# Expert layer: choice of the first two tiles stretched by 1.3 and moved apart, gate products later, row products on a straighter curve

## What is computed

```python
qh = (x2 @ w_q).reshape(t, 8, 2, 128)
scores = einsum('thcd,hckd->thck', qh, sub_keys)          # 8 heads x 2 halves x 128 keys
sv, si = top_k(scores, 16)
cand = sv[..., 0, :, None] + sv[..., 1, None, :]          # 16 x 16 sums for each head
cv, ci = top_k(cand, 16)                                  # 16 experts for each head
experts = i1 * 128 + i2                                   # of 16384
gates = softmax(cv)
act = gelu(einsum('tkd,td->tk', expert_u[experts], x))
out = einsum('tk,tkd->td', act * gates, expert_v[experts])
```

## Time and profile before

| | |
|---|---|
| Median of 3 runs | 3953.37 us (3952.84 to 3953.43) |
| Profiled execution, its own time | 3957.06 us |
| Its span, first to last instruction | 3955.3 us |
| Mean granted TensorE clock | 0.990 |
| TensorE matmuls | busy 3844.4 us, 97% |
| TensorE weight loads | 85% |
| VectorE | busy 2453.7 us, 62% |
| ScalarE | 39% |
| GpSimd | 14% |
| Up-projection stage | about 740 to 1500 us of the span |

### The profile page before, as it was taken

One profiled execution on the slowest core, in us unless ns is written; L12 is line 12 of the kernel. 1 busy time (PEld: TensorE's weight loads), 2 busy tenths in 40 slices (PEclk: granted clock), 3 DMA queues, 4 the chain that ended last, 5 costly groups with the idle time before them and its releaser, 6 DMA issues. The chain is left out here.

```text
span 3955.3 us, 53100 instructions
## 1 busy us (share of the span) xinstructions
PE 3844.4 (97%) x21989; PEld 3357.1 (85%) x21989; DVE 2453.7 (62%) x3730; ACT 1531.9 (39%) x2178; POOL 550.4 (14%) x405
## 2 busy tenths in 40 slices
PE   8999998998999999999999999999999999999998
PEld 7778887788999999999988887788888887688887
DVE  6433478699889767778775525765444542685443
ACT  3211345324766753333342226543222233644222
POOL 1000101101233333343311100110001010001000
PEclk9999999999999999999999999999999999999999
DMA  3344135335898999999944443332223434143332
GB/s 128 110 129 159 47 106 182 112 112 189 275 319 295 350 347 350 354 358 358 354 178 151 133 138 110 113 111 96 96 96 107 141 130 146 67 143 101 97 99 81
DMA packets 294188, 689.52 MB, mean 174 GB/s; under 512 B 19731, under 2 KB 77459, under 8 KB 277052
## 3 DMA queue, kind: packets, MB, share of 16 engines
q1 hardware_dynamic: 247868, 526.72, 39.4%
q0 software_dynamic: 36864, 134.23, 9.7%
q10 hardware_dynamic: 9216, 25.17, 1.6%
HBM read 585.11 MB, written 100.96 MB: 173 GB/s over the span
## 5 line engine op out<-in xcount | busy, mean ns | idle before, releaser
L1328 ACT CAST pe_w_high<-pe_w_raw 128x2048 fp32r<-128x2048 f32 (+1 forms) x168 | 316.4, 1883 | 601.7 <-DMA pe_w_raw<-in_peer_v_units 347.8
L1420 DVE TENSOR_TENSOR pe_w_low<-pe_w_raw,pe_w_high 128x2048 fp32r<-128x2048 f32 (+1 forms) x168 | 382.2, 2275 | 269.2 <-ACT pe_w_high L1328 269.0
L1215 PE MATMUL ps<-xn_p_high,pe_w_high 128*128 128x384 f32 (+1 forms) x1088 | 379.9, 349 | 17.7 <-DVE pe_w_low L1420 16.5
L2335 ACT CAST tail_w_high<-tail_w_raw 128x2048 fp32r<-128x2048 f32 (+3 forms) x124 | 221.4, 1790 | 442.0 <-DMA tail_w_raw<-in_w_in 144.5
L2344 DVE TENSOR_TENSOR tail_w_low<-tail_w_raw,tail_w_high 128x2048 fp32r<-128x2048 f32 (+3 forms) x124 | 266.7, 2155 | 184.5 <-ACT tail_w_high L2335 184.2
L1215 PE MATMUL ps<-xn_p_low,pe_w_high 128*128 128x384 f32 (+1 forms) x1088 | 371.1, 341 | 0.0
L1215 PE MATMUL ps<-xn_p_high,pe_w_low 128*128 128x384 f32 (+1 forms) x1088 | 371.0, 341 | 0.0
L1245 PE MATMUL ps<-pe_far_hidden_high,pe_w_high 128*128 128x384 f32 x1024 | 342.7, 335 | 0.0
L1245 PE MATMUL ps<-pe_near_hl,pe_w_high 128*128 128x384 f32 x1024 | 342.1, 334 | 0.0
L1245 PE MATMUL ps<-pe_far_hidden_high,pe_w_low 128*128 128x384 f32 x1024 | 342.1, 334 | 0.0
L1633 POOL DMA_INDIRECT home_pe_row<-in_peer_u,pe_expert x128 | 174.6, 1364 | 558.7 <-DVE pe_act L1606 361.6
(11 more groups left out here) (649 smaller groups left out, 9069.3 us busy)
## 6 DMA issues: line engine op xcount, KB each, us to landing
pe_w_raw<-in_peer_u_units SPq DMA_DIRECT2D x64, 1024.0 KB, 7.3
pe_w_raw<-in_peer_v_units SPq DMA_DIRECT2D x64, 1024.0 KB, 7.9
in_w_raw<-in_w_in SPq DMA_DIRECT2D x34, 1024.0 KB, 5.7
tail_w_raw<-in_w_up SPq DMA_DIRECT2D x32, 1024.0 KB, 5.5
tail_w_raw<-in_w_down SPq DMA_DIRECT2D x32, 1024.0 KB, 5.0
pe_w_raw<-in_w_in SPq DMA_DIRECT2D x28, 1024.0 KB, 5.0
tail_w_raw<-in_w_in SPq DMA_DIRECT2D x28, 1024.0 KB, 4.9
dram_peer_hidden<-pe_rings_r ACTq DMA_DIRECT2D x64, 384.0 KB, 5.8
```

The source lines that it names most:

```text
L1215: last = pe.matmul(ps[:, q, 0:n], w[:, s, at], xp[:, 4 * i + c, 0:n], start=(i == 0 and c == 0 and p == 0), stop=(i == 1 and c == 3 and p ...
L1328: act.copy(ring.flat(hi, u), ring.flat(raw, u)).then_inc(w_hi, 1)
L1420: dve.tensor_tensor(ring.flat(lo, u), ring.flat(raw, u), ring.flat(hi, u).bitcast(F32), ALU.subtract).then_inc(w_lo, 1)
L2335: act.copy(hi, raw).then_inc(self.w_hi, 1)
```

## The change

It changes seven planned numbers, or forms of them, and splits one semaphore.

- The choice of tile 0 begins at start(8) + 82 instead of + 70 (180.0 instead of 168.0 planned). Tile 3 stays at 128.0.
- Tiles 3 and 0 get the pace 1.3 instead of 1.0, and the exponentials follow the pace: 28.4 behind the start of the choice instead of 22 for tiles 3 and 0, 46.4 instead of 50 for tiles 1 and 2.
- The gate iterations run from 231.0 to 670.4 planned, 9.35 apart, instead of from 206.0 to 666.0, 9.79 apart. Through them tile 1's choice moves from 262.6 to 280.6 and tile 2's from 419.2 to 430.2, and the stores of the table move along.
- The exponent in `DOT` is 0.9 instead of 0.8: of the 128 row products, more come early and fewer late.
- `gate_stored` becomes two semaphores, one for each output buffer, with the waits on it rewritten.

`turns` is not among the changed lines. The due times of the units, of the loads, of the low halves and of the sums of rows stay. The whole diff:

```diff
--- before.py
+++ after.py
@@ -1030,13 +1030,14 @@
     ORDER = (3, 0, 1, 2)
     TURNED = [m for m in ORDER if m * P < N_DENSE]
     N_TURNS = len(TURNED)
-    PICK = {3: start(8) + 30.0, 0: start(8) + 70.0}
-    GATE = lambda it: PICK[0] + 38.0 + (start(D0) - 46.0 - PICK[0] - 38.0) / n_gates * it
+    PICK = {3: start(8) + 30.0, 0: start(8) + 82.0}
+    GATE = lambda it: PICK[0] + 51.0 + (start(D0) - 42.0 - PICK[0] - 51.0) / n_gates * it
     PER_BURST, N_BURSTS = BURST // UNIT, N_DENSE // BURST
     for m in (1, 2):
         PICK[m] = GATE(16 * m) - 100.0
+    PACE = {3: 1.3, 0: 1.3, 1: 2.3, 2: 2.3}
     first_dot, first_sum = PICK[3] + 55.0, start(D0) + 5.0
-    DOT = lambda j: first_dot + (first_sum - 20.0 - first_dot) * (j / PASSES) ** 0.8
+    DOT = lambda j: first_dot + (first_sum - 20.0 - first_dot) * (j / PASSES) ** 0.9
     SUM = lambda j: first_sum + (start(N_UNITS) - 28.0 - first_sum) / PASSES * j
     PASS = lambda n: DOT(n) if n < PASSES else SUM(n - PASSES)
 
@@ -1048,8 +1049,8 @@
     pick, c_val_a, c_cut, c_val_b, c_top = (sem(n) for n in ("pick", "c_val_a", "c_cut", "c_val_b", "c_top"))
     shifted, raised, ready, turned, kept_T = (sem(n) for n in ("shifted", "raised", "ready",
                                                                            "turned", "kept_T"))
-    away, one_j, gated, gate_made, gate_kept, gate_stored = (sem(n) for n in ("away", "one_j", "gated", "gate_made",
-                                                                               "gate_kept", "gate_stored"))
+    away, one_j, gated, gate_made, gate_kept = (sem(n) for n in ("away", "one_j", "gated", "gate_made", "gate_kept"))
+    gate_stored = [sem(f"gate_stored{s}") for s in range(2)]
     h_in, g_in = [sem(f"h_in{s}") for s in range(H_SLOTS)], [sem(f"g_in{s}") for s in range(2)]
     h_scaled, h_hi, h_lo, summed = (sem(n) for n in ("h_scaled", "h_hi", "h_lo", "summed"))
     x_sum, x_var, x_root, x_rstd, x_scaled, x_hi, x_lo, evicted_v = (
@@ -1148,7 +1149,7 @@
                             quads = slice(part * n // QUAD, (part + 1) * n // QUAD)
                             sp.dma_start(table.rearrange("u p (b x) -> p u b x", x=QUAD * BURST)[:, quads, b, :],
                                          gate_out[b % 2][:, part * n:(part + 1) * n, :].rearrange("p (u i) t -> p u (i t)", i=QUAD)
-                                         ).then_inc(gate_stored, 16)
+                                         ).then_inc(gate_stored[b % 2], 16)
 
                 def hidden_loads():
                     for e in range(N_DOWN):
@@ -1166,7 +1167,8 @@
                     for n in range(N_DOWN // 2):
                         yield start(D0 + 2 * n - (3 if n else 2)) + 1.5
                         if n == 0:
-                            sp.wait_ge(gate_stored, 16 * STORES * N_BURSTS)
+                            for stored in gate_stored:
+                                sp.wait_ge(stored, 16 * STORES * N_BURSTS // 2)
                         if n >= 2:
                             sp.wait_ge(h_scaled, 2 * n - 2)
                         sp.dma_start(gt[n % 2][:, :], table[n]).then_inc(g_in[n % 2], 16)
@@ -1351,7 +1353,7 @@
 
                 def softmax():
                     for i, m in enumerate(ORDER):
-                        yield PICK[m] + (50.0 if m in (1, 2) else 22.0)
+                        yield PICK[m] + 18.0 * PACE[m] + 5.0
                         act.wait_ge(shifted, i + 1)
                         act.activation(ej, ej, ACT.Exp).then_inc(raised, 1)
 
@@ -1361,7 +1363,7 @@
                         act.wait_ge(gate_made, n + 1)
                         b, t0 = n // (2 * PER_BURST), 4 * (n % (2 * PER_BURST))
                         if t0 == 0 and b >= 2:
-                            act.wait_ge(gate_stored, 16 * STORES * (b - 1))
+                            act.wait_ge(gate_stored[b % 2], 16 * STORES * (b // 2))
                         act.copy(gate_out[b % 2][:, :, t0:t0 + 4], ps[:, 4 + n % 3, :].rearrange("p (t i) -> p i t", t=4)).then_inc(gate_kept, 1)
 
                 def ones_j():
@@ -1451,7 +1453,7 @@
                 def choose():
                     v = Chain(dve, pick)
                     for order, m in enumerate(ORDER):
-                        at, pace = PICK[m], (2.3 if m in (1, 2) else 1.0)
+                        at, pace = PICK[m], PACE[m]
                         yield at
                         n = PH * order
                         dve.wait_ge(top, 64)
```

## The result

| | before | after |
|---|---|---|
| Median of 22 runs each | 3953.59 us (3951.18 to 3955.85) | 3959.11 us (3957.08 to 3960.97) |
| Profiled execution, its own time | 3957.06 us | 3958.78 us |
| Its span | 3955.3 us | 3957.0 us |
| Mean granted TensorE clock | 0.990 | 0.990 |

The ratio is 1.0014, with a 95% interval of 1.0008 to 1.002: 5.5 us slower, 0.14%. That lies on the side of the forecast and inside the 0.2% that counts as no change, and it is about half of the 10.3 us forecast. The lines of the kernel after are numbered two higher than those before in these functions.

A forecast was written before the change was run, and what follows sets the result against it. TensorE is busy for 97% of the span, so time can only be won where it idles or runs slowly. Terms 3.6 + 2.5 + 2.6 - 1.4 + 3.0 = +10.3 us on the 3953.4 median gave 3963.7 us, range 3951 to 3974.

The forecast's parts named there:

- tiles 3 and 0, slow clock included: Choices of tiles 3 and 0: net +3.6 us from the later `ready`, plus +2.5 for half clock after the long idle.
- tile 1: Choice of tile 1: low half of unit 34 late by 2.4 us, unit 35 by 2.0; +2.6 us (0 to +5).
- tile 2: Choice of tile 2: low half of unit 48 late by 5.5 us, unit 49 by 0.5; -1.4 us (-4 to +2).
- tail of the gates: Last gate products and stores: first gate table load leaves up to 6 us later; cost 0 to 6, taken as +3.
- The order in VectorE's queue: VectorE's queue walked: 2.52 us idle gone, unit 21's low half done at 966.0, tile 0's `ready` at 981.4.
- The step that decides: Tile 0's transposes keep their place in TensorE's queue, now ahead of `ready`; TensorE waits some 12 us, net +3.6 us.
- rival in which the stretch works: `ready` given before TensorE reaches tile 0's transposes, so the idles there go: -12.7 us, 3940.7 us; chance 0.08.
- The slow spell of 2.5: TensorE at half clock after the long idle before tile 0's transposes: +2.5 us.
- rival in which the tail slips whole: Fourth store behind load 71, table load behind it: all 6 us count, slow spell follows; +15.8 us, 3969.2; chance 0.08.
- At nothing: Split `gate_stored`, moved `Exp`, shifted row gathers and first products: no cost.
- likeliest case: The prediction's own case: +10.3 us, 3963.7 us, its terms' bounds giving 3957 to 3970; chance 0.60.
- case of no change: Wait for `ready` just pays back the idles it replaces, no slow spell, tail costs nothing: around 3957 us; chance 0.24.

The follow-up runs named there:

- e8_split: Kernel before with only the split `gate_stored` semaphores and the new due times of the exponentials; 3952.36 us, +0.1 against before.
- e3: Kernel after with the exponent of the row products back at 0.8; 3955.33 us.
- e4: Kernel after with the gates' end back at 46 instead of 42 ahead of the first down unit; 3967.38 us (five runs).
- e5: Kernel before with the row-product exponent 0.9 alone; 3959.03 us, +6.8 against before.
- e11: e1 with the exponent of the row products back at 0.8; 3950.65 us.
- e12: e10 with the exponent of the row products back at 0.8; 3945.54 us.
- e1: Kernel after with tile 0's transposes due 46 instead of 37 into its choice; 3951.32 us.
- e6: Kernel after with tile 1's choice due 1.4 us earlier; 3962.92 us.
- e10: Kernel after with tile 0 at pace 1.45, begun 1 us later; transposes at 50, gates 4, first row product 30, tile 2's choice 2 us later; 3945.01 us.
- e2: Kernel after with tile 0's transposes due 32.5 instead of 37 into its choice; 3961.54 us.

## Why the prediction was right or wrong

| term | forecast | profile, against before | against e8_split |
|---|---|---|---|
| tiles 3 and 0, slow clock included | +6.1 | +5.7 | +5.6 |
| tile 1 | +2.6 | +1.5 | +1.7 |
| tile 2 | -1.4 | -3.2 | -0.5 |
| tail of the gates | +3 | -0.5 | -0.9 |
| sum | +10.3 | +3.5 | +5.9 |

**The order in VectorE's queue**: right. Idle at unit 15 gone, unit 21 at 966.2 on the scale of before (966.0), the transposes at 981.3 (981.4), 11.27 us of idle in front of them (12). The pause of VectorE was forecast as 3.1 us at low 18; it was 2.1 there and 1.0 at low 19.

**The step that decides**: right, and tested. With the transposes moved the time falls by 8.0 us, the lost idle is 7.1. The rival in which the stretch works is out: `ready` came where the walk had it.

**The slow spell of 2.5**: right in place and size. The clock of 0.65 from 979 to 987 us makes 0.35 x 8 = 2.8 us (1.9 in the balance, which leaves out the transposes themselves), where the earlier trace rows had 1.00 behind the 2.89 us idle. The first quarter of unit 21 went slowly too, but ahead of a wait, and that cost nothing (in e3 it went at full clock, and the wait was longer by as much). The place as a whole came to +5.7 against +6.1.
The Trainium skill (TensorE: Matmul & The Clock Gate, What's actually happening) has idleness put the array at half clock. The 11.27 us idle agrees, with 0.65 behind it, and of the shorter ones only some do (last section).

**Tile 1**, +2.6: over by 1.1. Unit 34 waited 0.33 us (forecast 2.4) and unit 35 1.84 (2.0). Against that, the second one drew a slow spell of 1.3 (1120 to 1125 us, clock 0.66), which the forecast had not put in.

**Tile 2**, -1.4: the gain was 3.2. Unit 48 waited 3.48 (5.5), unit 49 0.39 (0.5). In both tiles the first of the two units came 2 us better than the count. The counts themselves were right; their starts were not. VectorE's timeline of the kernel after, where the two choices begin and at the low half of unit 48 (that of unit 34 is shown above, at 1106.11):

```profile
1038.56 0.28 DVE L1463 CAST pe_far_sif<-pe_far_si 128x256 f32<-128x256 uint32 x1
...
1193.70 0.28 DVE L1463 CAST pe_far_sif<-pe_far_si 128x256 f32<-128x256 uint32 x1
...
1258.07 2.29 DVE L1422 TENSOR_TENSOR pe_w_low<-pe_w_raw,pe_w_high 128x2048 fp32r<-128x2048 f32 x1
```

From the start of the choice to the end of that low half VectorE works 69.8 us in tile 1 (counted 70.1) and 66.7 in tile 2 (66.9), without a pause and with the low halves, selections and rows that were counted. But TensorE was ready for unit 34 at 1108.11, planned as 347.9, so the start planned as 280.2 stands for 1040.4, and the choice began at 1038.56; in the same way tile 2's 429.0 stands for 1195.5, and it began at 1193.70. Both starts were put 1.8 us too late. Of the 3.2 in tile 2, besides, 1.3 are slow spells, of which the kernel before had more in this one execution: against e8_split the gain is 0.5, and the forecast lies between the two.

**The tail**, +3: this is the term that failed, and the largest error of the sum. The path to the table load was right, even to the bound: the order turned as described and it left 5.7 us later. What failed is "from there the old distances hold: 11.1 us to the scaling". With the 6.2 us that it took, the same sum gives 24.4 + 6.2 + 4.0 = 34.6 us behind unit 68's start, against 34.5 at which TensorE wants it: 0.1. SyncE's rows say why. Before, the table load left 2.1 us behind the load of the first down unit and 1.6 behind that of its hidden values (SyncE's queue of the kernel before):

```profile
1482.54 0.34 SPq L1134 DMA_DIRECT2D pe_w_raw<-in_peer_v_units  x1
1483.01 0.39 SPq L1163 DMA_DIRECT2D pe_near_h<-dram_peer_hidden  x1
```

After, it left 6.9 us behind that load (1484.80). The DMA engines are at a share of 1.01 and 1.02 from 1480 to 1500 us in the two kernels, and I read the rows so that the table load lands when the bytes ahead of it are through, and an issue some microseconds later changes that little. The other kernels agree. In the four with the old order (before, e4, e5, e8) it leaves 0.4 to 1.9 us behind the hidden load and takes 10.7 to 12.2 us; in the ten with the new one it leaves 6 us or more behind it and takes 6.2 to 7.3. The exponent shows no effect on this of its own: with 0.8 and the new order it takes 6.3 (e3), 7.3 (e11) and 6.2 (e12). All this is read from rows; no kernel moved that load alone. The rival in which the tail slips whole is out, though the fourth store did not overtake load 71: it was issued behind it, and all 5.7 us of the later issue were there.

**At nothing**: right (e8). But the row products had been counted only as a part of the walk and of tiles 1 and 2, and alone they cost the kernel before 6.8 us.

**The sum**: 3.5 us by the profiles and 5.5 by the medians, against 10.3. The tail is 3.5 to 3.9 us of the difference, tile 1 about 1; tile 2 lies on either side of its term by which profile one takes for before. The 2 us between profiles and medians are the slow spells that the profiled execution of before had and e8_split had not. The range of 23 us held the result with ease, and the forecast of 3963.7 was 4.6 us too high. The likeliest case had the right mechanism in its largest term. The case of no change had the size, and one of its reasons, that the tail costs nothing; its other two failed: a slow spell did follow, and the wait for `ready` does not just pay back the old idles, since e1 gets 8.0 us back by moving the transposes.

## What to carry to other kernels

Where due times sort in-order queues, a producer that is moved or stretched needs every consumer's slot moved with it: look for consumers whose due time is a number of their own, since one line left behind cost 8 us here. After that look at pairs: a block of work due 0.1 or 0.2 us before a piece that TensorE waits for costs nearly its whole length (4.3 us more idle time for a block of 4.6, e6), so put the urgent piece first with some margin. And what is saved in one place can come back in another (5.73 against 5.77 us in tile 2, tile 1 in e10, the tail in e11 and e12), so an idle that is only redistributed is no gain. Last, where the effect is 0.1% of the time, one profile of each kernel is not enough to size a term: take a second one of the kernel before, or of a kernel known to run like it.

## What the runs showed of the hardware

- The time from issue to landing is no constant of a transfer: the same 768 KB table load took 10.7 to 12.2 us in the four kernels where it left within 2 us of the 384 KB hidden load ahead of it, and 6.2 to 7.3 in the ten where it left 6 us or more behind it, with DMA shares near 1. (Taken from the issue to the scaling that waited for it.)
- After a short idle of one and the same length the clock falls in one kernel's profiled execution and not in another's. Tile 2's 1.97 us idle has 0.68 behind it in before (1261 to 1266) and 1.00 in e8_split (1258 to 1263), two kernels of the same speed. Units 35 and 48 waited 1.84 and 3.48 us in after and 1.84 and 3.49 in e1; after has 0.66 behind both, 0.34 x 5 = 1.7 us lost each (rows 1120 to 1125 and 1260 to 1265 above). The windows of e1_turn46 behind the same two:

```profile
1115.00:1120.00 5.00, 4.90 (x31) 4.91 (x32) 5.00 (x14) 1.62 (x5) 1.26 (x2) 1.00 1.01 330
1253.00:1258.00 5.00, 4.71 (x28) 4.71 (x29) 5.00 (x14) 0.67 (x3) 1.06 (x2) 1.00 1.01 352
```

  The 2.18 us idle before unit 13, on the other hand, has 0.66 behind it in all eight kernels whose windows I took. What tells them apart stays open. For a sum of microseconds it means that such an idle costs its length and either nothing or up to 1.7 us more, and that one profile against another is uncertain by some of these.
- The length of a long idle did not matter for what follows: behind 21.85 us (e2) no more clock was lost than behind 11.27 (after).
